# Sums of a modulation vector: one ahead of each of sixteen products in place of two ahead of each of eight

## The reference, cut to what matters

```python
silu_c = jax.nn.silu(c)
mod_l = jnp.split(silu_c @ w_mod[l] + b_mod[l], 6, axis=-1)
hl = modulate(rms_norm(xl, norm1_g[l]), mod_l[0], mod_l[1])
zl = hl @ w_in[l] + b_in[l]
...
zkv = hc @ w_in[l, :, K_OFF:G_OFF] + b_in[l, K_OFF:G_OFF]
...
xl = xl + mod_l[2][:, None, :] * mixer_output(zl, y_na_l, *branch_params)
hl2 = modulate(rms_norm(xl, norm2_g[l]), mod_l[3], mod_l[4])
xl = xl + mod_l[5][:, None, :] * sq_relu_ffn(hl2, ...)
```

## Time and profile before

| | |
|---|---|
| time, median of 3 runs | 3089.54 us (3086.67 to 3093.76) |
| time of the profiled execution | 3094.16 us |
| its span in the trace | 3092.4 us |
| PE busy | 3044.7 us, 98% of the span |
| DVE busy | 1978.9 us, 64% |
| DMA | 561.31 MB, mean 182 GB/s |

### The profile page before, as it was taken

How to read it: one execution, slowest core, us unless ns; L and a number is a source line. 1 busy time by engine, 2 the same in 40 slices (tenths; PEclk the granted TensorE clock), 3 DMA queues, 4 the chain that set the end, 5 groups by cost and what they waited for, 6 DMA issues and landing times.

```text
span 3092.4 us, 49849 instructions
## 1 busy us (share of the span) xinstructions
PE 3044.7 (98%) x21871; PEld 2740.9 (89%) x21883; DVE 1978.9 (64%) x2957; ACT 331.0 (11%) x643; POOL 63.2 (2%) x121
## 2 busy tenths in 40 slices
PE   6999999999999999999999999999999999999998
PEld 3688844498899999999999999999999998898998
DVE  1039974554266577766666777776667575996665
ACT  1021000023130000111110000001002102000010
POOL 0000000020000000000000000000000000000000
PEclk9999999999999999999999999999999999999999
DMA  8999866673345565755555555555445654553443
GB/s 278 306 307 303 276 235 254 249 191 123 123 137 165 173 188 172 184 175 166 193 165 162 166 164 170 171 160 180 139 137 156 200 170 130 150 148 111 120 152 110
DMA packets 580038, 561.31 MB, mean 182 GB/s; under 512 B 24269, under 2 KB 548128, under 8 KB 570349
## 3 DMA queue, kind: packets, MB, share of 16 engines
q1 hardware_dynamic: 550656, 467.69, 49.1%
q0 software_dynamic: 11552, 80.90, 7.2%
q10 hardware_dynamic: 17613, 9.52, 1.2%
HBM read 549.56 MB, written 8.51 MB: 180 GB/s over the span
## 4 chain that ended last, share of the span: by engine, by line
PE 91%; DMA 4%; DVE 4%; issue 0%; ACT 0%; ACTq 0%; SPq 0%; DVEq 0%; POOLq 0%
PE psum L484 39%; PE psum L464 23%; PE psum L763 4%; PE psum L624 2%; PE psum L562 2%; PE psum L884 2%; PE psum L893 2%; PE psum L894 2%; PE psum L887 2%; PE psum L892 2%; PE psum L882 2%; PE psum L879 2%; DMA ring<-w_in 1%; DMA ring<-w_mod 1%; PE psum L937 1%; DVE arena L1942 1%
## 5 line engine op out<-in xcount | busy, mean ns | idle before, releaser
L464 PE MATMUL psum<-arena,ring 128*128 128x256 f32 (+2 forms) x3712 | 875.1, 395 | 0.6 <-ACTq L1183 0.6
L464 PEld LDWEIGHTS psum<-arena,ring 128*128 128x128 f32 x3712 | 698.5, 190 | 151.5 <-issue 64.9
L484 PE MATMUL psum<-arena 128*128 128x128 f32 x6144 | 702.8, 275 | 0.3 <-DVE arena L1767 0.3
L484 PEld LDWEIGHTS psum<-arena 128*128 128x128 f32 x6144 | 694.4, 192 | 7.2 <-issue 6.2
L484 PE MATMUL psum<-arena,ring 128*128 128x128 f32 x4224 | 486.1, 275 | 0.0
L484 PEld LDWEIGHTS psum<-arena,ring 128*128 128x128 f32 x4224 | 479.1, 192 | 0.7 <-issue 0.5
L1755 DVE TENSOR_TENSOR arena<-ring 128x2048 f32<-128x2048 f32 x96 | 220.1, 2292 | 273.7 <-PE psum L484 264.7
L1894 DVE SCALAR_TENSOR_TENSOR arena<-arena,cvec 128x2048 f32<-128x2048 f32 x60 | 141.0, 2350 | 87.0 <-DMA arena<-w_mod 86.1
L1736 DVE TENSOR_TENSOR arena<-ring,arena 128x1024 f32<-128x1024 f32 (+1 forms) x168 | 167.3, 996 | 5.3
L1736 DVE TENSOR_TENSOR arena<-arena 128x512 f32<-128x512 f32 (+7 forms) x257 | 134.3, 523 | 15.8 <-DVE arena L2658 5.7
L2515 DVE TENSOR_TENSOR arena<-ring 128x1024 f32<-128x1024 f32 x64 | 78.4, 1226 | 90.2 <-PE psum L879 89.4
(11 more groups left out here) (330 smaller groups left out, 2929.9 us busy)
## 6 DMA issues: line engine op xcount, KB each, us to landing
ring<-w_ff SPq DMA_DIRECT2D x128, 1024.0 KB, 5.7
ring<-w_in SPq DMA_DIRECT2D x88, 1024.0 KB, 7.6
arena<-w_mod POOLq DMA_DIRECT2D x64, 1024.0 KB, 6.3
ring<-ab_w_in SPq DMA_DIRECT2D x56, 1024.0 KB, 5.7
ring<-cd_w_in SPq DMA_DIRECT2D x48, 1024.0 KB, 5.8
ring<-w_mod SPq DMA_DIRECT2D x32, 1024.0 KB, 7.5
ring<-w_in SPq DMA_DIRECT2D x32, 512.0 KB, 5.0
ring<-w_o SPq DMA_DIRECT2D x16, 1024.0 KB, 5.7
```

Source lines behind the costliest of these rows:

```text
L464: mm = pe.matmul(psum[:, s, m * N:(m + 1) * N], w[:, k, m * P:(m + 1) * P], x(k)[:, 0:N], start=(j == 0), stop=(j == kt - 1))
L484: return pe.matmul(o, z, w, **kw) if tokens else pe.matmul(o, w, z, **kw)
```

## The change

In `k` the sixteen sums go one ahead of each of the 16 products of tile 3, in place of two ahead of each of the first eight. In the first half of `v` they go one ahead of each of the products `4 * s + k` = 5 to 8, in place of two ahead of each of the products 5 and 6: they begin at the same product and end eight products later. In the second half of `v` they go one ahead of each of the 16 products of the last tile, in place of two ahead of each of its last eight: they begin eight products earlier and end at the same product. Those of `sv` stay.

```diff
             def ahead_of_k(q, k):
 
-                if q == 3 and k < 8:
-                    mod_sum(7, 2 * k)
-                    mod_sum(7, 2 * k + 1)
+                if q == 3:
+                    mod_sum(7, k)
...
                         for t in range(4):
-                            if half == 0 and s == 1 and 1 <= k <= 2:
-                                mod_sum(7, 8 * (k - 1) + 2 * t)
-                                mod_sum(7, 8 * (k - 1) + 2 * t + 1)
-                            elif half == 1 and s == 3 and k >= 2:
-                                mod_sum(3, 8 * (k - 2) + 2 * t)
-                                mod_sum(3, 8 * (k - 2) + 2 * t + 1)
+                            if half == 0 and 5 <= 4 * s + k <= 8:
+                                mod_sum(7, 4 * (4 * s + k - 5) + t)
+                            elif half == 1 and s == 3:
+                                mod_sum(3, 4 * k + t)
```

## The result

The change makes the kernel slower: 3109.07 us median (7 runs) against 3092.24 us (7 runs), ratio 1.0052, 95% interval 1.0043 to 1.0062. That is 16 us by the ratio and 16.8 between the medians. The forecast had the sign, at 3102 us with a range up to 3106; the time lies 3 us above that range. The profiled execution took 3109.07 us, with a span of 3107.3 us.

The account below looks back on a forecast made before the run. PE was taken as the bound, 91% of the chain of waits. Terms 0.3 + 10.0 + 1.7 + 0.5 = +12.5 us, on the median 3089.54, make 3102 us; range 3092 to 3106.

Parts of the forecast that it names:

- The sums: On PE, 48 moved sums each cost 0.006 us more singly than in pairs, judged from `sv`: +0.3 us.
- the fast rival: On PE, single sums hide more weight loads: up to 10.7 us gained, 3080; chance 0.03, weaker case 0.02.
- The end of the sums in `k`: Last sum 6.9 us later, chunk transfers delayed, PE waits 11.3 us on line 2008 in place of 1.3: +10.0 us.
- T2: Second chunk transfer ahead of line 2008: issued at 445.0 beside ACT's 512 KB and SP's 1 MB, taking 9.6 to 11 us.
- T4: Fourth chunk transfer ahead of line 2008: issued behind `kept`, moving nothing until near 464, landing at about 468.
- the first rival: In `k`, the fourth chunk transfer gets ahead of `kept`; line 2008 at 465.5, total +5.7 to +7.4 us; chance 0.18.
- equal shares: In `k`, the fourth chunk transfer and `kept` share, half rate each; line 2008 at 466.6, total +8.5 us; chance 0.12.
- The sign of over 7 us of idle time: Sign of the held transfers: DVE's last addition ahead of line 2008 idle for more than 7 us.
- T3: Third chunk transfer ahead of line 2008: issued at 450.7, between the second and fourth, holding up nothing more.
- The clock: Behind PE's wait on line 2008, one stretch at the 1.2 GHz level: +1.7 us, bounds 0 and 3.4.
- The sums in `v`: Additions end later and second-half sums are due earlier, so PE waits for `mod_added`: +0.5 us, bounds 0 and 3.
- the rigid 0.9 us: In `v`, additions moved rigidly end at 606.9, sum due at 605.95 + 0.1: a wait of up to 0.9 us.

Follow-up runs that it names:

- e2: Against the kernel before, only the sums in the first half of `v` go singly; ratio 1.0001 (one 6417 us execution left out).
- e3: Against the kernel before, only the sums in the second half of `v` go singly, beginning eight products earlier; ratio 1.0007.
- e15: The whole change run once more under the profiler, one execution; `k` part 93.43 us, `v` part 119.61 us.
- e1: Against the kernel before, only the sums of `k` go one ahead of each of sixteen products; ratio 1.0036.
- e5: Against the kernel before, the sums of `k` stay two each but ahead of the last eight products of tile 3; ratio 1.0033.
- e7: Against the kernel before, sums of `k` spread and ACT writes `kept` after tile 6 in place of tile 4; ratio 1.0028.
- e4: Against the kernel before, the sums in both halves of `v` go singly, those of `k` unchanged; ratio 1.0005.
- e9: Against the kernel before, sums of `k` spread and two of DVE's six chunk additions moved behind the reads of line 2008; ratio 1.0004.
- e11: Against the kernel before, only two of DVE's six chunk additions moved behind the reads of line 2008, no sums spread; ratio 0.9997.
- e14: Second repeat under the profiler of both halves of `v` spread, `k` as before, one execution; `k` part 81.32 us, `v` part 119.32 us.
- e8: Against the kernel before, first half of `v` spread, second half's sums beginning four products later than in the change; ratio 1.0000.

## Why the forecast was too low

**The sums.** Forecast +0.3 us; measured 0.0 (e2, e3). Taking the 256-column products of `sv` as a stand-in was 0.006 us a sum too dear. Nothing of the fast rival came. The weight loads fit that, first those of the kernel before around the row, then those of the kernel after:

```profile
522.12 0.19 PEld L763 LDWEIGHTS psum<-ring,arena 128*128 128x128 f32 x1 [0.24 <-issue]
...
522.98 0.19 PEld L674 LDWEIGHTS psum<-ones,arena 128*128 128x128 f32 x1 [0.24 <-issue]
```

```profile
422.56 0.19 PEld L674 LDWEIGHTS psum<-ones,arena 128*128 128x128 f32 x1 [0.24 <-issue]
422.99 0.19 PEld L674 LDWEIGHTS psum<-ones,arena 128*128 128x128 f32 x1 [0.24 <-issue]
```

While a product runs, one load of what follows it comes early. A pair has one of its four loads early (522.98) and a single sum one of its two (422.56). But a pair leaves one product without sums, and there that product's own load has the place (as at 522.12). So in two periods two loads come early in either arrangement.

**The end of the sums in `k`.** Line 1904 was forecast for 440.6 and came at 438.52 + 2.05 = 440.57. T2 was given 9.6 to 11 us and took 9.47. Line 2008 was forecast 10.0 us late and came 9.05 late. One link in between came out otherwise in this execution: T4 was to be issued behind `kept`, and the text named an earlier issue as a sign that the forecast fails. Issues of SP, ACT and POOL after, in answer to the earlier trace rows:

```profile
442.87 0.42 ACTq L1188 DMA_DIRECT2D arena<-sgu_b  x1
...
442.95 31.32 SPq L366 DMA_DIRECT2D ring<-w_in  x2
...
455.43 0.53 POOL L1620 DMA_DIRECT2D arena<-w_mod  x1 [5.97 <-DVE arena L1891]
...
455.84 0.36 ACTq L1188 DMA_DIRECT2D kept<-arena  x1
```

T4 goes out 0.41 us ahead of `kept`, the condition of the first rival, and is held up all the same. DMA queues of the kernel after from 459.5 to 465 us (packets, MB, share), in answer to the earlier trace rows:

```profile
q10 hardware_dynamic: 115, 1.88, 79.8%
q0 software_dynamic: 78, 0.51, 23.0%
```

`kept` moves 1.88 MB while POOL's queue moves 0.51. That lies between the forecast (nothing moves) and equal shares. By the rule of the Trainium skill, "DMA: Bandwidth & Descriptors" (section "Queues, rings and completion order"), both queues are served in turn. The trace agrees where both move: from 460 to 463 us it has 51 packets of `kept` and 49 of POOL's queue, 0.84 and 0.40 MB. In the earlier trace rows one of them moved nothing for five us; whether it had work then no trace shows.

The order of T4 and `kept` isn't the same each time. In e15, the same kernel, T4 went out 0.05 us behind `kept`, as forecast:

```profile
459.07 0.36 ACTq L1188 DMA_DIRECT2D kept<-arena  x1
...
459.12 0.53 POOL L1620 DMA_DIRECT2D arena<-w_mod  x1 [6.51 <-DVE arena L1891]
```

From 461 to 463 us only the queue of `kept` moved there, 0.80 MB, and T4 landed 10.02 us after its issue. In e1 and e5 it went out 0.13 and 0.17 us behind. These three waits are 11.12, 11.04 and 11.09 us, against 10.37 where T4 was ahead, and on the scale of before line 2008 starts at 470.4 us in all three (forecast 470.6). So the mechanism in `k` was right, and its sign too strict: either order costs the same to 0.7 us, and which one comes hangs on some tenths of a us. The sign of over 7 us of idle time ahead of DVE's last addition didn't come (5.08 us, with T3's addition in between). That `kept` has 5 us of the wait is shown by e7.

**The clock.** Forecast +1.7 us for one fall behind the wait; 11.26 - 9.05 = 2.2 us measured, net of the second wait of 0.29 us in the kernel before, which is gone.

**The sums in `v`.** This is the step that failed: "+0.5" for the wait for `mod_added`, with nothing for the clock behind it, where the profiled execution lost 5.69 us. The account was right: the additions end later, the sums are due earlier, and only together do they use up the margin (e2, e3, e4). Two sizes were off. The wait is 2.0 to 2.7 us, not 0.5. The additions took 617.25 - 549.16 = 68.1 us from line 1904 to their end, against 66.9 before, and the forecast had set the rigid 0.9 us down, to 0.5, where it should have gone up. And the fall of the clock was priced for `k` only, though the earlier trace rows show one behind a wait of 1.60 us. In `v` a fall was seen in three of six executions and cost up to 3.4 us, as each us at the lower level loses half.

**The level.** The forecast added its step to 3089.54 us, the median of three runs; over seven it is 3092.24. Of the 7.1 us between 3102 and 3109.07 this is 2.7; `v` is 5.2, `k` with its sums -0.7, as the two profiled executions have it. They are one case: against 81.32 and 117.08 us, the usual parts of the kernel before, the change loses 18.3 us in its profiled execution and 14.6 in e15, of which `v` is 5.7 and 2.5 and `k` 12.6 and 12.1 (forecast 12.0 with the sums). How much of the 16.8 us between the medians is due to `v` isn't shown.

## What to carry to other kernels

A short product placed between long ones cost the same here wherever it stood, 0.22 us, so its place is to be chosen by who waits for its result. Here eight products later made the last sum 7 us late and DVE 4.6 us, and the additions behind it then sent a transfer out together with two others, so that 5 us became 9. Where one edit moves a producer later and another its consumer earlier, the margin between them is spent twice and must be checked for both at once.

A wait of PE is to be priced with the clock behind it, even a wait of 2 us. And a stall of this kind may be cured in the list of the engine that is waited for: four additions ahead of the reads in place of six took away the loss in `k` with the late sums left as they were (e9).

## What the runs showed of the hardware that was not expected

- Waits of PE of the same length, 2.0 to 2.7 us, were followed by a granted clock of 0.50 for 6.8 us, 3.4 us, or not at all; one of 2.07 us was, one of 2.29 us wasn't.
- A transfer of POOL issued 0.41 us ahead of one of ACT finished behind most of it: 9.73 us from issue to landing, while ACT's queue moved 1.88 MB and POOL's 0.51 from 459.5 to 465 us. While both moved, their packets were equal in number, 51 and 49, and not in bytes.
- The stretch from the first sums of `k` to the end of `v` repeats to 0.02 us between executions where no wait hangs on a transfer (198.40 in e9 and e11, 198.41 in e2). From there to the end all kernels take 2469.1 us. The spread of the whole times comes from ahead of it: the product of line 581 starts between 416.86 us (e14) and 426.42 us (e8), though nothing was edited there. So a change here is read better from the stretch than from the whole time.
